# High and low part of x side by side in SBUF: two of the three split matmuls of each weight tile become one of 512 columns

## What is computed

```python
def rmsnorm(x, g):
    y = x * rsqrt(mean(x * x, -1) + EPS)
    return y * g

def hybrid_mixer(x, ...):            # GDN + MoBA
    proj = rmsnorm(x, norm_g) @ w_in         # 2048 -> 7184
    qkv_a = silu(causal_dwconv(qkv_a, gdn_conv_w))   # four taps
    ...
    return concat(o_a, o_b) @ w_out

def conv_ffn(x, ...):
    h = rmsnorm(x, norm_g)
    gate = causal_dwconv(h @ w_gate, conv_w) + conv_b   # three taps
    return (silu(gate) * (h @ w_up)) @ w_down

def _mamba2_mixer(x, ...):
    zxbcdt = x @ w_in                        # 2048 -> 10304
    xbc = silu(conv(xbc, conv_w) + conv_b)           # four taps
    ...                                      # chunked state space, gate z, group norm
    return y @ w_out

def _swa_mixer(x, k, v, ...):
    proj = x @ w_in                          # q and gate, 2048 -> 4096
    ...
    return (o * silu(gate)) @ w_out
```

## Time and profile before

| | |
|---|---|
| runs of the kernel, us | 2731.27, 2741.95, 2742.14; median 2741.95 |
| the profiled execution, us | 2732.62 |
| its span, us | 2730.8 (1.8 less) |
| mean granted clock of TensorE | 0.976 of full speed |
| busy | TensorE 2580.5 us (94%), VectorE 1744.2 (64%), ScalarE 1206.1 (44%), GpSimd 359.3 (13%) |
| HBM read | 410.80 MB; DMA queue of the loads busy 47% |

### The profile page before, as it was taken

The page is one execution under the profiler, slowest core; times in us unless marked ns, Lnnn a source line. Parts: engine busy times, 40 slices in busy tenths (PEclk is TensorE's granted clock), DMA queues, the critical chain, the costliest instruction groups (busy, mean ns, idle before and its releaser), DMA issues. The chain is left out here.

```text
span 2730.8 us, 51941 instructions
## 1 busy us (share of the span) xinstructions
PE 2580.5 (94%) x21076; PEld 2500.9 (92%) x21076; DVE 1744.2 (64%) x2727; ACT 1206.1 (44%) x1886; POOL 359.3 (13%) x529
## 2 busy tenths in 40 slices
PE   3999999998889999999999989999999999799997
PEld 2999999998879999999999989999999988799997
DVE  1766655566456665665666677767777776466765
ACT  3333324344344444444444544444444443455553
POOL 1122120023010000000001201110101112210002
PEclk7999999999999999999999999999999999799998
DMA  5432334554335556656556544445444444244452
GB/s 130 168 109 93 109 109 148 169 175 155 126 124 186 182 182 174 204 172 200 185 168 192 182 161 149 152 151 173 159 160 158 147 142 152 93 147 147 141 168 86
DMA packets 125375, 418.36 MB, mean 153 GB/s; under 512 B 13780, under 2 KB 18644, under 8 KB 125012
## 3 DMA queue, kind: packets, MB, share of 16 engines
q1 hardware_dynamic: 125140, 415.05, 47.0%
HBM read 410.80 MB, written 3.67 MB: 152 GB/s over the span
## 5 line engine op out<-in xcount | busy, mean ns | idle before, releaser
L1498 DVE TENSOR_TENSOR WL<-WR,WH 128x1024 fp32r<-128x1024 f32 (+3 forms) x811 | 968.0, 1196 | 541.0 <-ACT WH L1128 537.5
L679 PE MATMUL b<-XH,WH 128*128 128x256 f32 x4224 | 1232.1, 292 | 42.1 <-ACT WH L1128 22.9
L680 PE MATMUL b<-XL,WH 128*128 128x256 f32 x4224 | 1201.8, 285 | 0.0
L681 PE MATMUL b<-XH,WL 128*128 128x256 f32 x4224 | 1201.5, 284 | 0.0
L1128 ACT ACTIVATE WH<-WR 128x1024 fp32r<-128x1024 f32 (+3 forms) x811 | 811.2, 1010 | 555.6 <-PE b L681 521.1
L679 PEld LDWEIGHTS b<-XH,WH 128*128 128x128 f32 x4224 | 816.2, 193 | 59.2 <-issue 27.5
L680 PEld LDWEIGHTS b<-XL,WH 128*128 128x128 f32 x4224 | 817.7, 194 | 4.0 <-issue 3.3
L681 PEld LDWEIGHTS b<-XH,WL 128*128 128x128 f32 x4224 | 816.6, 193 | 0.0
L679 PE MATMUL b<-OH,WH 128*128 128x256 f32 x1680 | 481.0, 286 | 14.7 <-DVE XT L1659 10.5
L680 PE MATMUL b<-OL,WH 128*128 128x256 f32 x1680 | 469.2, 279 | 0.0
L681 PE MATMUL b<-OH,WL 128*128 128x256 f32 x1680 | 469.0, 279 | 0.0
(11 more groups left out here) (359 smaller groups left out, 2204.7 us busy)
## 6 DMA issues: line engine op xcount, KB each, us to landing
WR<-a_w_in SPq DMA_DIRECT2D x160, 512.0 KB, 3.6
WR<-w_in SPq DMA_DIRECT2D x112, 512.0 KB, 3.6
WR<-w_gate SPq DMA_DIRECT2D x88, 512.0 KB, 3.7
WR<-w_up SPq DMA_DIRECT2D x88, 512.0 KB, 3.5
WR<-a_w_out SPq DMA_DIRECT2D x64, 512.0 KB, 3.5
WR<-b_w_in SPq DMA_DIRECT2D x64, 512.0 KB, 3.7
WR<-w_down SPq DMA_DIRECT2D x64, 384.0 KB, 3.5
WR<-w_down SPq DMA_DIRECT2D x64, 320.0 KB, 3.1
```

Of the source, the lines that this page charges most:

```text
L679: mm(ps, WH[:, slot, at:at + P], xh, start=(k == 0), stop=False)
L680: mm(ps, WH[:, slot, at:at + P], xl, start=False, stop=False)
L681: m = mm(ps, WL[:, slot, at:at + P], xh, start=False, stop=(k == p["kt"] - 1))
L1498: dve.tensor_tensor(WL[:, s, 0:n], WR[:, r, 0:n], WH[:, s, 0:n].bitcast(F32), ALU.subtract).then_inc(*dve_w.up(i))
```

## The change

It puts the high and the low part of each x tile side by side, `XX[P, 16, 2, S]`, 2,048 bytes per tile. For an x product TensorE then runs two matmuls per tile k in place of three: one of 512 columns with the high weights over both parts, whose results fall into columns 0 to 255 and 256 to 511 of the bank, and one of 256 columns with the low weights over the high part, added onto columns 0 to 255. In the last tile of a product the two change places. The bank's second half has to be added to the first: ScalarE copies it to a new buffer `low` (two of 256 columns), VectorE adds the first half to it there, and the evacuation proper reads `low` in place of the bank. The bank is free after that addition (`dve_lo`). The products over `OH`, `OL` and `OX` are computed as before, and so are the two narrow products of `x` (`ba` and `dt`, 16 and 64 rows).

SBUF is laid out anew: `WR`, `WH`, `WL`, `XT`, then a tensor `apart` of 48 fp32 (192 bytes) that nothing uses, `XX`, `OH`, `OL`, `OX`, the scratch tensors, and `par` and `con` behind them. From `XX` to `OX` everything begins 192 bytes on from `WH` and `WL` modulo 512. The one-hot table of the relative bias leaves `con` and is loaded by a DMA of its own. The diff, cut:

```diff
@@ number
+        if isinstance(p["src"], int):
+            p["w"], self.wide = self.wide, self.wide + 1
@@ program
-    XT = sb("XT", [P, 16, S])
-    XH = sb("XH", [P, 16, S], F32R)
-    XL = sb("XL", [P, 16, S], F32R)
     WR = sb("WR", [P, RAW, CK * P])
     WH = sb("WH", [P, HL, CK * P], F32R)
     WL = sb("WL", [P, HL, CK * P], F32R)
-    par = sb("par", [P, PN])
-    con = sb("con", [P, CN])
+    XT = sb("XT", [P, 16, S])
+    sb("apart", [P, 48])
+    XX = sb("XX", [P, 16, 2, S], F32R)
     OH = sb("OH", [P, 16, S], F32R)
     OL = sb("OL", [P, 16, S], F32R)
...
+    low = sb("low", [P, 2, S])
@@ half_of
             if k0 == 0 and p["prior"]:
-                w.wait_ge(*dve_ev.of(p["prior"]))
+                w.wait_ge(*(dve_lo if "w" in plan.products[p["prior"]] else dve_ev).of(p["prior"]))
...
-                mm(ps, WH[:, slot, at:at + P], xh, start=(k == 0), stop=False)
-                mm(ps, WH[:, slot, at:at + P], xl, start=False, stop=False)
-                m = mm(ps, WL[:, slot, at:at + P], xh, start=False, stop=(k == p["kt"] - 1))
+                wh, wl, end = WH[:, slot, at:at + P], WL[:, slot, at:at + P], k == p["kt"] - 1
+                if by[0] != "x":
+                    mm(ps, wh, xh, start=(k == 0), stop=False)
+                    mm(ps, wh, xl, start=False, stop=False)
+                    m = mm(ps, wl, xh, start=False, stop=end)
+                else:
+                    if end:
+                        mm(ps, wl, xh, start=False, stop=False)
+                    m = mm(both, wh, XX[:, k, :, :].rearrange("p a b -> p (a b)"), start=(k == 0), stop=end)
+                    if not end:
+                        m = mm(ps, wl, xh, start=False, stop=False)
@@ scalar, evac
-            v = version(key)
+            v, p = version(key), plan.products[key]
+            if "w" in p:
+                w.wait_ge(*pe_prod.of(key))
+                if p["w"] > 1:
+                    w.wait_ge(*dve_ev.of(wide_keys[p["w"] - 2]))
+                act.activation(low[:, p["w"] % 2, :], banks[p["bank"]][:, S:2 * S], ACT.Copy).then_inc(*act_lo.up(key))
...
             if key[0] == "wg":
-                w.wait_ge(*pe_prod.of(key))
+                w.wait_ge(*dve_lo.of(key))
...
-                act.activation(T1(8), banks[plan.products[key]["bank"]][:, 0:S], ACT.Tanh, scale=0.5).then_inc(
+                act.activation(T1(8), low[:, p["w"] % 2, :], ACT.Tanh, scale=0.5).then_inc(
@@ vector, evac
             w.wait_ge(*pe_prod.of(key))
+            if "w" in p:
+                hi, ps = ps, low[:, p["w"] % 2, :]
+                w.wait_ge(*act_lo.of(key))
+                dve.tensor_tensor(ps, ps, hi, ALU.add).then_inc(*dve_lo.up(key))
+                w.wait_ge(*dve_lo.of(key))
```

More of the change, by code:

```diff
@@ L87, in constants @@
     oh[32] = n < 0
-    put("onehot", oh)
-    return c
+    return c, oh.astype(np.float32)
 class Signal:
@@ L174, in __init__ @@
         self.late = True
-        self.convs = self.gates = self.big = 0
+        self.convs = self.gates = self.big = self.wide = 0
         self.bigs = []
@@ L480, in program @@
     WL = sb("WL", [P, HL, CK * P], F32R)
-    par = sb("par", [P, PN])
-    con = sb("con", [P, CN])
+    XT = sb("XT", [P, 16, S])
+    sb("apart", [P, 48])
+    XX = sb("XX", [P, 16, 2, S], F32R)
     OH = sb("OH", [P, 16, S], F32R)
     OL = sb("OL", [P, 16, S], F32R)
+    with nc.sbuf_tensor("OX", [P, 12, S], F32R) as OX:
+        pass
+    t2x = sb("t2x", [P, 6, 512])
+    t2s = sb("t2s", [P, 12, 512])
+    t1s = sb("t1s", [P, 10, S])
     KM = sb("KM", [P, 4, S])
@@ L488, in program @@
     ACC = sb("ACC", [P, S])
-    t2s = sb("t2s", [P, 12, 512])
-    t1s = sb("t1s", [P, 10, S])
+    par = sb("par", [P, PN])
+    con = sb("con", [P, CN])
     cvs = sb("cvs", [P, 3, S + 4])
@@ L495, in program @@
     posb = sb("posb", [P, S], I32)
-    with nc.sbuf_tensor("OX", [P, 12, S], F32R) as OX:
-        pass
-    t2x = sb("t2x", [P, 6, 512])
+    low = sb("low", [P, 2, S])
     banks = [ctx.enter_context(nc.psum_tensor(f"b{i}", [P, 512], F32)) for i in range(8)]
@@ L557, in x_last @@
         return plan.last_of[v]
+    wide_keys = [k for k, p in plan.products.items() if "w" in p]
     conv_keys = [k for k, p in plan.products.items() if p["evac"] == "conv"]
@@ L663, in half_of @@
             p = plan.products[key]
-            ps = banks[p["bank"]][:, 0:S]
+            both = banks[p["bank"]]
+            ps, both = both[:, 0:S], both[:, :]
             slot = i % HL
             if k0 == 0 and p["prior"]:
-                w.wait_ge(*dve_ev.of(p["prior"]))
+                w.wait_ge(*(dve_lo if "w" in plan.products[p["prior"]] else dve_ev).of(p["prior"]))
             w.wait_ge(*act_w.of(i))
@@ L707, in toep @@
             w.wait_ge(*ld_con.of("con"))
-            w.wait_ge(*ld_rel.of("rel"))
+            w.wait_ge(*ld_rel.of("onehot"))
             to = free(("toep", "t", "t"))
-            mm(to[0:8, 0:384], relp[:, :], cc("onehot", 0, 384, 33), start=True, stop=True).then_inc(*pe_toep.up("t"))
+            mm(to[0:8, 0:384], relp[:, :], T2(16)[0:33, 0:384], start=True, stop=True).then_inc(*pe_toep.up("t"))
         def norm(v, name):
@@ L952, in dt @@
                 at = slice((k - c0) * P, (k - c0) * P + 64)
[L953 to L955 removed]
+                mm(to, WH[:, i % HL, at], XX[:, k, 0, :], start=(k == 0), stop=False)
+                mm(to, WH[:, i % HL, at], XX[:, k, 1, :], start=False, stop=False)
+                m = mm(to, WL[:, i % HL, at], XX[:, k, 0, :], start=False, stop=(k == 15))
             if k == 15:
```

27 lines of the change are left out of this document (13 added, 14 removed).

## The result

| | before | after |
|---|---|---|
| median of the runs, us | 2738.91 (2731.27 to 2742.14, 4 runs) | 2754.2 (2752.3 to 2754.66, 4 runs) |
| span of the profiled execution, us | 2730.8 | 2752.9 |

The ratio is 1.0059 with a 95% interval of 1.0034 to 1.0083: the change makes the kernel **slower by 0.6%**, against 2648 us forecast and a range of 2608 to 2698.

The account below looks back on a forecast made before the run. The prediction took TensorE's rate of 256-column matmuls, held by weight loads, as the bound. From 2732.6 us it took 130 off TensorE's path and added 45 of losses: 2648 us, range 2608 to 2698.

Parts of the forecast that it names:

- The bound: Whole kernel: bound by the rate at which TensorE takes a 256-column matmul, 0.120 us each.
- the 512-column rows: Profile rows of fp32 matmuls, two clocks per column: every 0.430 us against 427 ns of clocks, so 3 ns added.
- The placement: x products: starting at the weights' place modulo 512 costs 7 ns per matmul; 192 bytes apart gives 113 ns.
- The losses: Time the added evacuation takes back across the stages: 40 us summed, plus 5 for waits not found, 45.
- point 1: Four-tap convolution products: VectorE and ScalarE loop grows from 5.56 to 6.0 us, TensorE needs 5.27; six lose up to 4.4.
- points 1 and 2: Mamba stage, convolution loops and groups beside the previous group's state space: together 20 of TensorE's 39 us gain lost.
- point 3: Delta-rule stage: 3 us for the first six products and 3 for small steps waiting longer, 6 us lost.
- point 4: Gate and up: VectorE busy 8.4 of 10.54 us per pair, loop 10.2; 4 us lost over 44 pairs.
- point 5: Sliding window: VectorE busy 10.9 of 13.6 us per pair of products; 5 of the 16 us gain lost.
- columns, not loads: Rival for x matmuls: columns hold TensorE, so it gains nothing and the kernel slows to 2760 us; chance 0.06.
- the half-clock rows: Profile rows at 1.2 GHz: a 256-column matmul takes 0.21 us, one clock per column, so 107 ns at full clock.
- the 0.112 of bare loads: One-column fp32 matmuls: their weight loads come every 0.112 us, taken as what a weight load takes.

Follow-up runs that it names:

- wide_no_evac: The changed kernel with its 512-column matmul but without the copy and the addition, leaving out the low part's product; 2707.26 us, ratio 0.9893.

## Why the prediction was wrong

- **The bound.** That the kernel goes by TensorE's rate in the gate and up stage held. For the whole it was too simple: in the sliding window TensorE had no gap and still was not alone, as its pair stayed at 14.5 to 14.6 us when its matmuls got cheaper. (The 11.4 us of waits for weight splits are VectorE's; ScalarE's split of `WH` has 22.9 more in the earlier trace rows, one single wait.)
- **"So a 256-column fp32r matmul is held by the weight load of the next one": this step failed.** The floor of 111 ns exists, but 256 columns lie just above it, and what they pay is their columns, 107 ns, and 7 to 13 ns on top. The widths show it: 147, 173, 202 and 227 to 233 ns at 320, 384, 448 and 512 columns, where the columns alone outlast the 111 ns and 13 to 20 ns are still added, in place of the 3 that the prediction had where the load lies under the columns. What the 7 to 20 ns are, and whether the load has a part in them, stays open.
- **"The wide matmul takes 512 / 2.4 = 213 ns plus 3", from the 512-column rows, and "the narrow one ... 113": the terms that were mis-sized.** They measured 235 and 118. The rows used are fp32 matmuls with two clocks per column and show 3 ns on 427; fp32r ones show 14 to 20 on 213, and 22 before a narrow one. The gain was to be 31 ns per k and was 7: 4224 x 7 = 30 us in place of 130. wide_no_evac measured 27 under its before (2734.08).
- **The placement** was right as a cause, and 7 ns is its size at best: 64 bytes give 41 us (2736.93 - 2695.6) and the earlier trace rows's 113 ns in two thirds of the x matmuls. That x would have `OH`'s rate also behind a wide matmul was wrong. The Trainium skill (SBUF — State Buffer, Who interferes with whom) has TensorE never waiting for another engine at its SBUF ports. That is not contradicted, as the 120 ns stand with the other engines idle too. But it speaks of other engines and not of where an operand lies. That "by it the new layout is worth nothing" was the prediction's own conclusion, and it is wrong: the same instructions take 113 or 120 ns by the distance alone.
- **The losses:** 45 forecast, 47 measured (43 in the spans), but for the wrong places, so that the sum fits by luck. The loop of point 1 came out to the digit. VectorE's timeline in the Mamba stage, which answers to the earlier trace rows:

```profile
1832.78 1.23 DVE L1516 TENSOR_TENSOR WL<-WR,WH 128x1024 fp32r<-128x1024 f32 x1 [0.52 <-ACT WH L1141]
1833.92 0.41 DVE L1633 TENSOR_TENSOR low<-low,b 128x256 f32<-128x256 f32 x1
1834.37 0.42 DVE L1637 TENSOR_TENSOR cvs<-low,RB 128x256 f32<-128x256 f32 x1
1834.72 1.22 DVE L1516 TENSOR_TENSOR WL<-WR,WH 128x1024 fp32r<-128x1024 f32 x1
1835.85 1.52 DVE L1594 SCALAR_TENSOR_TENSOR t1s<-cvs,par,t1s 128x256 f32<-128x256 f32 x3
1837.86 0.43 DVE L1622 SCALAR_TENSOR_TENSOR t2s<-t1s 128x256 f32<-128x256 f32 x1 [0.48 <-ACT t1s L1212]
1838.81 1.23 DVE L1516 TENSOR_TENSOR WL<-WR,WH 128x1024 fp32r<-128x1024 f32 x1 [0.53 <-ACT WH L1141]
```

  From split to split 6.03 us, where 6.0 was forecast and 5.56 measured before; from the addition's start to that of VectorE's next step it is 1834.37 - 1833.92, the 0.45 that were added. The Mamba stretch lost 17 (726.3 - 709.2; points 1 and 2: 20), but 6 of it in five products at its start, which no point names; everything ahead of the gate and up stretch 7 (point 3: 6), though with three matmuls it is 2 (827.3 - 825.4), and such a difference is within the scatter; gate and up nothing (203.3 in both kernels; point 4: 4); the sliding window 15.6 (219.1 - 203.5; **point 5: 5**). Point 5 took VectorE's busy share (10.9 of 13.6) for its slack, where, as in point 1, the sum along the loop of engines was wanted.
- **The rival "columns, not loads"** came nearest: it gave 2760 and decided from 349 ns per k on; 353 and 2754 were measured. It had 0.06. It was right in what is paid, and near in the number partly by luck: its 120 ns for 256 columns wherever they lie are refuted by the 113, and it had 0 gained and 27 lost where 30 and 47 were measured. Against it stood the half-clock rows, which show only that the columns are clocked, and the 0.112 of bare loads, which show a floor and not that 256 columns lie on it. The rule named beside it in the Trainium skill (TensorE: Matmul & The Clock Gate, Back-to-back issue gap), N / 2.4 + 2.5 ns for the gap of an isolated matmul, has the right thing paying but not the size of this stream: 109 and 216 ns by the page, 113 to 120 and 227 to 235 here. None of the others came as it was stated: the added work of VectorE and ScalarE holds back the Mamba stage and the sliding window, not gate and up.
- **The sum with the measured terms:** 2732.6 - 30 + 47 = 2750, against the 2754 measured.

## What to carry to other kernels

A fixed cost per instruction is known only if a shape on either side of the one in question has been timed: here one extra width (384 columns) would have told columns from loads. Before merging two instructions, ask what the second one pays that the merged one does not; here two narrow ones took 227 ns at their best, and the merged one 235. Try the operands' distance in SBUF by itself: a filling of 64 bytes with the matmuls of before gave 1.3%, and three matmuls in the new layout 1.8%: **the fastest kernel of this study, 2683.65 us, ratio 0.9822 (0.9773 to 0.9870)**. And where a stage is full on TensorE, add up the other engines' loop through it before booking a gain or writing off a cost: the stage can be full on both.

## What was not expected of the hardware

- A matmul of 256 fp32r columns takes 113 to 120 ns by the distance of its moving operand from the weights modulo 256 bytes, with the other engines idle; at 192 bytes the same weights again or new ones make no difference (113.3 and 113.4). 512 columns take 227 where 256 are slowest (distance 0) and 233 where 256 are fastest (192).
- At a distance of 192 bytes three 256-column matmuls run at 113.4 or at 117.7 ns each, and keep to one of them through a whole run of matmuls. A 512-column matmul with a 256-column one takes the slower one's sum (353 = 3 x 117.7) in most tiles, 85% of them in the changed kernel.
- VectorE's reduction over two halves of a bank (512 elements in, 256 out) takes 0.684 us, the addition with one half from SBUF 0.416, ScalarE's copy of 256 columns 0.378 on average.
